# Key blocks of a block-sparse decode step: scored one by one as they arrive, or held in SBUF, summed for the gate and scored where selected

## The reference

```python
k_full = cache_k[page_table[:, :own_first]].astype(f32).reshape(Bd, n_full, MOBA_BLOCK, H, D)
kmean = jnp.mean(k_full, axis=2)
gate = jnp.einsum('bhtd,bnhd->bhtn', qf, kmean)
_, sel = lax.top_k(gate, topk)
...
kg = cache_k[pages, :, hidx].reshape(Bd, H, T, topk * MOBA_BLOCK, D)
vg = cache_v[pages, :, hidx].reshape(Bd, H, T, topk * MOBA_BLOCK, D)
s = jnp.einsum('bhtd,bhtkd->bhtk', qf, kg.astype(f32)) * scale
```

## Time and profile before

| | us |
|---|---|
| median of 3 runs (563.67 to 565.16) | 564.84 |
| profiled execution, first to last instruction | 562.0 |
| TensorE busy | 439.0 |
| VectorE busy | 409.6 |
| GpSimd busy | 283.6 |
| ScalarE busy | 141.6 |

### The profile page before, as it was taken

The page is one execution under the profiler, slowest core; times in us unless marked ns, Lnnn a source line. Parts: engine busy times, 40 slices in busy tenths (PEclk is TensorE's granted clock), DMA queues, the critical chain, the costliest instruction groups (busy, mean ns, idle before and its releaser), DMA issues.

```text
span 562.0 us, 6963 instructions
## 1 busy us (share of the span) xinstructions
PE 439.0 (78%) x2048; PEld 208.0 (37%) x2048; DVE 409.6 (73%) x594; ACT 141.6 (25%) x307; POOL 283.6 (50%) x266
## 2 busy tenths in 40 slices
PE   0899989969959977767295876778649883999893
PEld 0443434324334443334142633434224432444340
DVE  0458989989999986978896879684776898332133
ACT  5302002101434343144303231324130220021012
POOL 5788748876874664575433556165633632000001
PEclk9899999979997899696758596858677995999898
DMA  8986786988986887566457755274558624132101
GB/s 294 315 302 225 282 321 206 347 259 288 333 273 166 256 271 219 167 201 181 107 153 229 217 170 173 83 219 150 171 203 287 197 41 165 31 67 92 39 3 40
DMA packets 89782, 108.79 MB, mean 194 GB/s; under 512 B 60736, under 2 KB 61248, under 8 KB 89744
## 3 DMA queue, kind: packets, MB, share of 16 engines
q0 software_dynamic: 18480, 67.25, 36.5%
q1 hardware_dynamic: 59632, 23.20, 15.4%
q10 hardware_dynamic: 11632, 17.90, 9.3%
HBM read 104.02 MB, written 4.28 MB: 193 GB/s over the span
## 4 chain that ended last, share of the span: by engine, by line
PE 53%; DVE 23%; issue 10%; ACT 6%; POOL 4%; ACTq 1%; DMA 1%; DVEq 0%; POOLq 0%
PE PA L671 25%; PE PA L760 9%; DVE sall L1033 9%; DVE prod L1175 5%; PE PO L734 3%; PE SM L623 3%; ACT junk L854 2%; POOL rstd L541 2%; PE PA L711 2%; PE TP L721 2%; PE DC L772 1%; PE SM L684 1%; DMA V<-in_page_table 1%; PE DC L786 1%; DVE vn L1070 1%
## 5 line engine op out<-in xcount | busy, mean ns | idle before, releaser
L526 POOL DMA_INDIRECT K<-in_cache_k,kidx x128 | 149.1, 1164 | 78.2 <-DVE prod L1175 52.3
L671 PE MATMUL PA<-wbuf,hT 128*128 128x512 f32 x384 | 187.3, 639 | 0.0
L596 POOL TENSOR_TENSOR pprod<-K,qb 128x1024 f32<-128x1024 f32 x43 | 101.1, 2352 | 37.3 <-DVE sall L1033 36.9
L1175 DVE TENSOR_TENSOR prod<-K,qb 128x1024 f32<-128x1024 f32 x85 | 112.7, 1342 | 7.6 <-ACT qb L988 7.5
L671 PEld LDWEIGHTS PA<-wbuf,hT 128*128 128x128 f32 x384 | 75.7, 206 | 94.5 <-issue 94.3
L1033 DVE TENSOR_REDUCE sall<-prod 128x16 f32<-128x1024 f32 x85 | 100.9, 1206 | 0.0
L540 POOL TENSOR_SCALAR rstd<-msum 128x1 f32<-128x1 f32 (+3 forms) x25 | 6.5, 261 | 148.5 <-ACT junk L854 77.0
L760 PE MATMUL PA<-wbuf,hT 128*128 128x512 f32 x128 | 60.1, 624 | 0.0
L1033 DVE TENSOR_REDUCE sall<-pprod 128x16 f32<-128x1024 f32 x43 | 51.9, 1208 | 1.2 <-POOL pprod L596 1.2
L950 ACT ACTIVATE pr<-pr,smax 128x128 f32<-128x128 f32 (+3 forms) x32 | 18.0, 562 | 134.7 <-DVE smax L1125 129.6
L711 PE MATMUL PA<-kT,qT 64*128 64x128 f32 (+3 forms) x64 | 28.9, 536 | 11.2 <-ACT vn L917 7.3
(11 more groups left out here) (177 smaller groups left out, 462.7 us busy)
## 6 DMA issues: line engine op xcount, KB each, us to landing
V<-in_cache_v SPq DMA_DIRECT2D x366, 32.0 KB
wbuf<-in_w_in ACTq DMA_DIRECT2D x5, 2048.0 KB, 11.8
wbuf<-in_w_in SPq DMA_DIRECT2D x2, 2048.0 KB, 13.7
wbuf<-in_w_out ACTq DMA_DIRECT2D x2, 2048.0 KB, 8.4
K<-in_cache_k,kidx POOLq DMA_INDIRECT x128, 5.6
ya<-in_x_prompt SPq DMA_DIRECT2D x2, 512.0 KB, 4.6
yb<-in_x_prompt SPq DMA_DIRECT2D x2, 512.0 KB, 8.1
out<-yb SPq DMA_DIRECT2D x4, 256.0 KB
```

The lines of the kernel that those rows point to most:

```text
L526: pool.indirect_dma_start(K[:, m % SLOTS, :, :].rearrange("p r w -> p (r w)"), None, k_rows, bass.IndirectOffsetOnAxis(ap=kidx[:, b, n:n + ...
L596: pool.tensor_tensor(pprod[:, :, :], K[:, m % SLOTS, :, :], qb[:, b % 2, :].unsqueeze(1).broadcast_to([P, 2, W]), ALU.mult).then_inc(s_pmu ...
L671: last = pe.matmul(PA[n % 2][:, :], lhs, rhs, start=(kc == 0), stop=(kc == KC - 1))
L1175: dve.tensor_tensor(prod[:, slot, :, :], K[:, m % SLOTS, :, :], qb[:, b % 2, :].unsqueeze(1).broadcast_to([P, 2, W]), ALU.mult).then_inc(s ...
```

## The change

K gets 16 slots, one for each block of one row. GpSimd adds the two positions of every block (`sum_rows`, 512 elements), with VectorE having none of these sums (`of_dve` is False). Per four blocks TensorE adds up the 128 partitions with a shifted one-column window (gs) into one PSUM bank. VectorE multiplies that with q, sums, transposes and takes the three largest (ga), finds their pages (pg), and then multiplies q only with the selected 128x128 pieces of K, 24 per row, whose place it reads from registers (ex, in four parts). One reduction (sr) makes the scores. The next row's loads start when the last of the 24 multiplies is done, five at once and then one per block. V has one buffer instead of two, in two halves of heads that pv0 and pv1 free; SyncE fetches it from pg on and stores each row's result behind pv1. The planner has other due times (a period of 43 instead of 39), and the sample's output steps stand before the prompt's last output tile. The core of the diff:

```diff
-SLOTS = 10
-POOL_SHARE = 3
-
-
-def of_pool(m):
-
-    return m % POOL_SHARE == 1
-
-
-def pool_count(m):
-
-    return sum(map(of_pool, range(m)))
-
-
-def sp_heads(b):
-
-    return SP_HEADS if b < B - 1 else SP_LAST
+SUMS = 6
+PARTS = 4
+LEAD = 5
+
+
+def of_dve(n):
+
+    return False
+
+
+def dve_sums(m):
+
+    return sum(of_dve(x % NB) for x in range(m))
+
+
+def pool_sums(m):
+
+    return m - dve_sums(m)
...
+        e = END_US + PERIOD_US * b
         for n in range(NB):
-            events.append((t + PERIOD_US * (n + 1) / NB, ("ks", b, n)))
-        e = t + PERIOD_US
-        chain = [(.01, ("dg", b)), (GT, ("gt", b)), (BC, ("bc", b)), (MT, ("mt", b)), (MB, ("mb", b)),
-                 (PVD, ("pvd", b))]
-        events += [(e + dt, s) for dt, s in chain]
-        for k, h in enumerate(range(sp_heads(b), H)):
-            events.append((e + BC + .1 + FV * k, ("fv", b, h)))
+            events.append((e - ARRIVE_US * (NB - 1 - n), ("ks", b, n)))
+        for g in range(G):
+            events.append((e - ARRIVE_US * (NB - 4 - 4 * g) + GS, ("gs", b, g)))
+        for dt, name in ((GA, ("ga", b)), (PG, ("pg", b)), (SR, ("sr", b)), (BC, ("bc", b)), (MT, ("mt", b)),
+                         (MB, ("mb", b)), (PV0, ("pv0", b)), (PV1, ("pv1", b))):
+            events.append((e + dt, name))
+        for i in range(PARTS):
+            events.append((e + EX + EX_STEP * i, ("ex", b, i)))
+        for i in act_ranks(b, 1):
+            events.append((e + 3 + FV * i, ("fv", b, i)))
         if b >= 1:
-            events.append((t - QB, ("qb", b)))
+            events.append((e - QB, ("qb", b)))
...
+END_US, PERIOD_US, ARRIVE_US = 38.0, 43.0, 1.5
+GS, GA, PG, EX, EX_STEP, SR, BC = 1.5, 3.0, 4.6, 4.5, 1.8, 13.0, 15.0
+MT, MB, PV0, PV1, QB, FV = 20.0, 26.0, 32.0, 52.0, 14.0, 9.0
...
-        K = sb("K", [P, SLOTS, 2, W])
+        K = sb("K", [P, NB, 2, W])
...
+        def sum_rows(eng, b, n, done):
+
+            eng.wait_ge(s_k[n], 16 * (b + 1))
+            if n < SUMS and b >= 1:
+                eng.wait_ge(s_scr, b)
+            if n in (4, 5) and b == 0:
+                wait_full(eng, tp_full, tp_use[("xs",)])
+            if n >= SUMS:
+                eng.wait_ge(s_gs, G * b + (n - SUMS) // 4 + 1)
+            eng.tensor_tensor(ksum[:, n % SUMS, :], K[:, n, 0, :], K[:, n, 1, :], ALU.add).then_inc(done, 1)
+
+        def wait_v_free(eng, b, hh):
+            if b >= 1:
+                eng.wait_ge(dc_full, dc_use[(f"pv{hh}", b - 1)] + 1)
...
+                if s[0] == "pg":
+                    b = s[1]
+                    sp.wait_ge(s_sel, b + 1)
+                    for hh in range(2):
+                        wait_v_free(sp, b, hh)
+                        fetch_v(sp, b, hh, [k for k in range(TOP) if k not in act_ranks(b, hh)], "vs")
+                if s[0] == "pv1":
+                    b = s[1]
+                    sp.wait_ge(dc_free, dc_use[s] + 1)
+                    for j in range(4):
+                        sp.dma_start(obs[b:b + 1, :].rearrange("b (t j d) -> b t j d", t=2, j=4)[:, :, j, :],
+                                     osb[32 * j:32 * j + 1, b % 2:b % 2 + 1, :].rearrange("a b (t d) -> a (b t) d", t=2)
+                                     ).then_inc(s_obs[b % 2], 16)
...
+                if s[0] == "ex" and s[2] == PARTS - 1 and s[1] < B - 1:
+                    pool.wait_ge(s_ext, s[1] + 1)
+                    for n in range(LEAD):
+                        load_k(NB * (s[1] + 1) + n)
                 if s[0] == "ks":
                     b, n = s[1], s[2]
-                    m = NB * b + n
-                    if of_pool(m):
-                        pool.wait_ge(s_k[m % SLOTS], 16 * (m // SLOTS + 1))
-                        pool.wait_ge(dc_free, dc_use[("qb", b)] + 1)
-                        if pool_count(m) >= 1:
-                            pool.wait_ge(s_red, score_no[m - POOL_SHARE] + 1)
-                        pool.tensor_tensor(pprod[:, :, :], K[:, m % SLOTS, :, :],
-                                           qb[:, b % 2, :].unsqueeze(1).broadcast_to([P, 2, W]), ALU.mult
-                                           ).then_inc(s_pmul, 1)
-                    if m + SLOTS - 1 < B * NB:
-                        load_k(m + SLOTS - 1)
+                    if not of_dve(n):
+                        sum_rows(pool, b, n, s_psum)
+                    if b >= 1 and n + LEAD < NB:
+                        load_k(NB * b + n + LEAD)
...
+                elif kind == "gs":
+                    b, g = s[1], s[2]
+                    pe.wait_ge(s_psum, pool_sums(NB * b + 4 * g + 4))
+                    pe.wait_ge(s_dsum, dve_sums(NB * b + 4 * g + 4))
+                    if g == 0 and b >= 1:
+                        pe.wait_ge(s_gate, b)
+                    for j in range(4):
+                        last = pe.matmul(GB[32 * j:32 * j + 32, :], win[:, 31 - g:63 - g],
+                                         ksum[:, (4 * g + j) % SUMS, :], start=(g == 0), stop=(g == G - 1),
+                                         tile_position=(0, 32 * j))
+                    last.then_inc(s_gs, 1)
...
+                        act.wait_ge(s_ext, b)
...
+                    if of_dve(n):
+                        sum_rows(dve, b, n, s_dsum)
...
+                    dve.wait_ge(s_gs, G * (b + 1))
+                    dve.wait_ge(dc_free, dc_use[("qb", b)] + 1)
+                    dve.tensor_tensor(sumq, GB[:, :], qb[:, :], ALU.mult).then_inc(s_gate, 1)
+                    dve.wait_ge(s_gate, b + 1)
+                    link(dve.tensor_reduce(g128[:, 0:H], sumq.rearrange("p (h d) -> p h d", h=H), AX.X, ALU.add))
+                    link(dve.transpose(gT[:, :], g128[:, :]))
+                    for j in range(4):
+                        last = dve.tensor_copy(g16[:, :, j], gT[32 * j:32 * j + H, 0:G])
+                    link(last)
+                    gates = g16[:, :, :].rearrange("h g j -> h (g j)")
+                    link(dve.max(top8[:, :], gates))
+                    link(dve.max_index(topi[:, :], top8[:, :], gates))
+                    if b >= 2:
+                        for hh in range(2):
+                            dve.wait_ge(s_v[hh], 16 * 4 * TOP * 2 * (b - 1))
+                    dve.tensor_copy(selw[0:H, 0:TOP], topi[:, 0:TOP])
                     link(dve.tensor_copy(vals[:, :, 0], topi[:, 0:TOP]))
+                    link(dve.transpose(selT[:, b % 2, :], selw[:, :]))
+                elif kind == "pg":
+                    b = s[1]
...
+                        dve.wait_ge(dc_full, dc_use[("bc", b - 1)] + 1)
+                    dve.tensor_tensor(spread[:, :, :], ident[0:H, 0:H].unsqueeze(2).broadcast_to([H, H, TOP]),
+                                      vals[:, :, 0].unsqueeze(1).broadcast_to([H, H, TOP]),
                                       ALU.mult).then_inc(s_spr, 1)
+                    link(dve.tensor_copy(selw[0:H, TOP:3 * TOP].rearrange("h (k j) -> h k j", j=2), vals[:, :, 1:3]))
+                    dve.transpose(selT[:, b % 2, :], selw[:, :]).then_inc(s_sel, 1)
+                elif kind == "ex":
+                    b, part = s[1], s[2]
+                    if part >= 1:
+                        dve.wait_ge(s_sel, b + 1)
+                    size = H * TOP // PARTS
+                    for x in range(size * part, size * (part + 1)):
+                        k, h = divmod(x, H)
+                        if h == 0:
+                            block_regs = [dve.alloc_register(f"blk{b}_{k}_{i}") for i in range(H)]
+                            dve.load(block_regs, selT[k:k + 1, b % 2, 0:H])
+                        n = dve.snap(block_regs[h], min_val=0, max_val=NB - 1)
+                        last = dve.tensor_tensor(kq[:, h * TOP + k, :, :],
+                                                 K[:, bass.ds(n, 1), :, h * HD:(h + 1) * HD]
+                                                 .rearrange("p a r d -> p (a r) d"),
+                                                 qb[:, h * HD:(h + 1) * HD].unsqueeze(1).broadcast_to([P, 2, HD]),
+                                                 ALU.mult)
+                        if h == H - 1:
+                            for r in block_regs:
+                                dve.free_register(r)
+                    if part == PARTS - 1:
+                        last.then_inc(s_ext, 1)
+                elif kind == "sr":
+                    b = s[1]
+                    dve.wait_ge(s_ext, b + 1)
+                    if b >= 1:
+                        dve.wait_ge(s_pex, b)
+                    dve.tensor_reduce(sc[:, :, :, :].rearrange("p h k r -> p (h k) r"), kq[:, :, :, :], AX.X,
+                                      ALU.add).then_inc(s_scr, 1)
```

284 lines of the change are left out of this document (109 added, 175 removed).

## The result

The changed kernel takes 636.32 us (median of 4 runs, 635.27 to 639.12) against 565.0 (563.67 to 568.37): a ratio of 1.124, 95% interval 1.119 to 1.129. It is 71 us slower, and 32 us slower than the 604 that I forecast; the range held it. The profiled execution took 637.03 us, of which 635.3 are its span; 1.7 us lie outside it.

A forecast was written before the change was run, and what follows sets the result against it. VectorE was taken to set the decode part's pace, TensorE's in-order queue coupling it to the prompt. Start 72.2, seven periods of 53.2, extras 49 and end 107.5 gave 601 us of span; with 2.8 outside, 604, range 562 to 642.

The forecast's parts named there:

- Start, 72.2 us: From the span's start to the end of row 0's first projection tile, its adds done before: 72.2 us.
- Period of 53.2 us: One row's serial loads and adds 38.1, gate sums 1.3, gate and multiplies 13.8 us; seven such periods.
- gate chain: VectorE's once-per-row work between last add and last multiply: gate, pages, 24 multiplies, register loads; 13.8 us with semaphores.
- Extras in the attention stages, 49 us: In-order waits beside the prompt's attention, rows 2 to 6: 1, 8, 16, 15, 9 us; bounds 15 and 65.
- VectorE's reduction (sr): Reduction over 3072 after the multiplies, beside five loads: 3.2 us, costing nothing unless over 2 us late.
- Last stretch, 107.5 us: After the last gate sums: remaining planned TensorE work 84.9 us plus transposes of y, folds, slow clock and output, together 107.5.
- Outside the span, 2.8 us: Median run time lies 2.8 us above the profiled span; added to the 601 us of span.
- TensorE's added work: 32 groups of four gate-sum matmuls at 1.3 us, 42 us in all; TensorE waits for GpSimd's adds.
- Rival 1: VectorE's relief removes the prompt's waits and the kernel gets faster, near 550 us; chance 0.13.
- Rival 2: Transfers bind: K's burst beside V's single buffer, 5 us more per period, about 640; chance 0.22 together with larger extras.
- Rivals 3 and 4: Savings cancel the loss, about 565 us; or the change does not do what it says, 0 GpSimd adds; chance 0.02.
- The second rule: Shared SBUF ports lock for a whole instruction: VectorE steps beside the 128 adds wait up to 1.2 us each, sum unchanged.

The follow-up runs named there:

- e4: Changed kernel, but GpSimd takes three branches' roots from early squares without waiting for ScalarE's squares (their scale is left out); 598.6 us.
- e9: Changed kernel with the edits of e4 and e6 together; 575.5 us.
- e12: Changed kernel with one planner constant altered: a row's gate is laid down every 49 us instead of 43; 665.0 us.
- e5: Changed kernel with every group of TensorE's gate sums issued twice; 647.3 us.
- e2: Changed kernel, but multiplies read a constant tile, so the next row's loads wait only for this row's adds, all issued ahead; 605.7 us.
- e1: Changed kernel with half of the adds, those of odd blocks, on VectorE instead of GpSimd; 614.9 us.
- e3: Changed kernel, but GpSimd copies the first row of each block instead of adding two; 604.6 us.
- e6: e1 with the two value steps planned later, at 40 and 54 us instead of 32 and 52; 603.3 us.
- e7: Changed kernel with all adds on VectorE and none on GpSimd; 619.5 us.
- e10: e9 plus the edit of e2 with 8 instead of 16 loads issued ahead; 556.2 us, work left out.

## Why the prediction was right, and where 32 us were missing

By the forecast's own sum, span to span: 601 forecast, 635.3 measured.

- *Start, 72.2 us*: 75.0 (+2.8). In e4, e9 and e12 the same stretch took 71.3, 70.4 and 71.5 us and in e5 78.4, so the 2.8 are not read.
- *Period of 53.2 us*: right for the stages without attention (54.8, 57.1, 53.4), and for the reason given, with two errors that partly cancel. The gate chain was 12.5 us, not 13.8: the multiplies follow each other at 0.21 us, though each lasts 0.29. The add was 1.28 us, not 1.2, and a pair of load and add 2.42, not 2.35, which is some 2 us a row. The first two periods had 1.6 and 3.9 us more than forecast; TensorE's waits for V there, 7.7 and 8.5 us at the value step, are the likely rest. e2 shows that most of what these periods lost hangs on the wait for the multiplies, and e1, e3 and e6 show what holds them when the adds are shortened.
- *Extras in the attention stages, 49 us*: this is the term that was mis-sized. Above 53.2 a period the measured extras are 1.6, 3.9, 0.2, 18.7, 22.5, 21.8 and 13.6, together 82.3, against 0, 0, 1, 8, 16, 15, 9. The mechanism was the one named: steps of GpSimd between the adds that wait for ScalarE's squares. In rows 3 to 6, between a row's first load and its last add, GpSimd stood 4.3, 9.7, 17.1 and 8.8 us for squares, 40 in all, and its rstd steps took 10 us themselves. What else there is, I had put at nothing: 4.6 us in row 4 for VectorE's reduction (sr), which was to cost nothing unless it came more than 2 us late; 4.0 us in row 3 for gate sums at the six slots; some 8 us more from gate to first load than in the first rows, and some 11 from last add to gate, 7 of them in row 3, where TensorE had prompt work in hand before the last gate sums. Row 3, priced at 8 us above the base, lost 18.7. The upper bound of this term, 65, was too low also; three of these periods are above the 60 to 70 us that were named, and the last gate came at 529.7 us, not near 490. e4 takes 31 us off the periods 3->4 to 6->7, and 45 us above the base stay there without GpSimd's wait for squares; these are named by no run of their own.
- *Last stretch, 107.5 us*: 105.6. The transposes of y that I set at 8 us behind VectorE's gate waited 7.2 us. The other parts were not read one by one.
- *Outside the span, 2.8 us*: 1.0. Both take a median from the span of another execution; the time less the span of one execution is 1.7 us, before and after.
- With the signs: 2.8 + 33.3 - 1.9 - 1.8 = 32.4 us over the forecast.
- *TensorE's added work*: 42 us by the forecast and 45.3 measured. The matmuls that went, which I left out, were 15 us. The sum goes by the serial chain and not by this work, and e9 and e10, with all of it, bear that out. The slower clock, some 17 us of TensorE's busy time, was in the forecast only as 3 us in the last stretch, in the price of the gate sums and in the upper bound of the extras; what it cost in time is not shown.
- *Rival 1, the relief of VectorE makes it faster*: refuted. It was relieved (226.7 us busy instead of 410), the time is longer, and e7, which gives it 83 us of adds, is faster than the changed kernel.
- *Rival 2, the transfers bind*: partly true. SyncE's fetch and stores of a row took 42 to 50 us, not the 53 I had counted, and each fetch ended before the next row's began; but V's arrival beside the burst held TensorE 7.7 and 8.5 us in the first two rows, and up to 16 in e1 and 20 in e7, once the adds were faster.
- *Rivals 3 and 4*: none of it; 128 adds stand on GpSimd.

I weighed one rule: two-input elementwise work belongs on VectorE (the Trainium skill, GPSIMD Engine Reference, section 4.1 Engine selection). The runs agree with it, in size too: the same add took 0.69 us on VectorE with none on GpSimd (e7), and 1.28 us on GpSimd. But following it to the letter (e7) was worth 17 us of 71. The estimate from the page's figure for 2048 elements had made an add 1.12 us; the measured 1.28 decides.

The second rule was that of the shared ports, where I left the sum as it was: VectorE steps beside the adds were to wait up to 1.2 us each. That bound was wrong. The sixteen steps on vn (ns, min/median/max), then four of them at a time: beside GpSimd's loads and adds in turn, beside adds back to back, and with no add; last GpSimd's line of the second time:

```profile
L1078 DVE SCALAR_TENSOR_TENSOR vn<-vn,rstd,gain x16: 338/346/7084, 264.7 to 360.3; 128x128 f32<-128x128 f32 x16
...
264.65 4.01 DVE L1078 SCALAR_TENSOR_TENSOR vn<-vn,rstd,gain 128x128 f32<-128x128 f32 x4 [3.02 <-POOL rstd L552]
...
295.15 8.89 DVE L1078 SCALAR_TENSOR_TENSOR vn<-vn,rstd,gain 128x128 f32<-128x128 f32 x4 [8.80 <-POOL rstd L552]
...
335.44 1.14 DVE L1078 SCALAR_TENSOR_TENSOR vn<-vn,rstd,gain 128x128 f32<-128x128 f32 x4 [7.46 <-POOL rstd L552]
```

```profile
297.74 6.14 POOL L427 TENSOR_TENSOR ksum<-K 128x512 f32<-128x512 f32 x5
```

A step is 0.34 us by itself. One of them took 7.08: it ended 0.2 us after the last of five adds that GpSimd made back to back. So such a step does not wait for one add but, here, for all that follow each other without a gap. That the pages call the ports an exclusive lock (the Trainium skill, SBUF — State Buffer, section "SBUF: two separate sides") fits these lines. The sixteen steps were 19.0 us in sum where the kernel before had 11.7, three of them at 2.43 beside a product. L1078 has 2% of the chain that ended last, and I had it at nothing; what the hold costs the kernel in time no run shows.

## What to carry to other kernels

When an edit takes work off the engine that sets the pace, ask first whether the buffers still let two rows overlap: here ten slots that ran on over the border of a row became sixteen that don't, and the work of a row, its loads, adds, gate and multiplies, came to stand one behind the other. A step that waits for another engine should not stand in the queue that feeds the critical chain: one wait of GpSimd for ScalarE's squares was worth 38 us in the changed kernel. Where several engines wait for each other in fixed order, a sum that follows one of them came out too low here, 49 us against 82. And TensorE's busy time is no constant of the work: the same matmuls were busy 485.9 us in the changed kernel and 466.4 in e4, at granted clocks of 0.823 and 0.854.
